# Routed experts in alternating order, with the work around their first items rearranged

## The chip, the core and the metric

The kernel runs on one NeuronCore of a Trainium2 chip. The metric is the device time of one execution in microseconds. Engines are named as in the profile: PE (TensorE, matmuls) with PEld (its weight loads), ACT (ScalarE), DVE (VectorE), POOL (GpSimd) and SP (SyncE, which here issues DMAs).

## The reference, cut to what matters

One layer over 1024 tokens of width 1024: normalised projection, a spatial gating half and a Fourier half, an output projection with the residual, then a mixture of experts:

```python
hn = rms_norm(h, norm2_g[l]).reshape(bsz * s, d)
eidx, gates = route(hn, w_router[l], router_bias[l])      # 8 of 64 experts for each token
routed = routed_experts(hn, eidx, gates, w_gate[l], w_up[l], w_down[l])
# for each expert e and its rows xb:
#   (silu(xb @ w_gate[e]) * (xb @ w_up[e])) @ w_down[e] * gate, added to the tokens' rows
shared = (jax.nn.silu(hn @ ws_gate[l]) * (hn @ ws_up[l])) @ ws_down[l]
h = h + (routed + shared).reshape(bsz, s, d)
return rms_norm(h, final_norm_g)
```

w_gate and w_up are 64 x 1024 x 256, w_down 64 x 256 x 1024, all float32. An expert's weights are 3 MB. The sum over experts does not depend on their order but for rounding.

## The kernel before

**Items.** The kernel counts the tokens of each expert on the chip and cuts each expert's rows into items of at most 128 rows. Table `tab` has two rows of integers, one column for each item: row 0 the item's expert, row 1 twice that number plus 1 if the item is the first of its expert. `ends` holds the number of turns; three items make a turn (`TURN`), and the loops over turns run to that number. With the inputs drawn there are 93 items of 64 experts.

**An item** i goes through these steps. POOL gathers 128 rows from the normed rows in DRAM into `Xg[u]` (L1514) and keeps each row's gate for the item's expert (L1524). PE transposes them (L456). ACT copies them to `xTh` in a rounded float format (L955) and DVE takes the remainder `xTl` (L1332). PE multiplies by gate and up into `ps[3]` in 24 matmuls (L715): high by high, high by rest, rest by high. ACT makes the silu `hs` (L950), DVE multiplies gate, silu and up into `hh` (L1325), PE transposes `hh` (L737), ACT copies `hTh` (L965), DVE takes the remainder `hTl` (L1337), and PE makes the down product in 12 matmuls (L729), which waits for `s_hl`, that is for hTl. ACT copies the result to `ob` (L961), and POOL adds it to the rows in DRAM by an indirect DMA (L1540). PE runs one item ahead: in item i it does the transposes of item i+1's rows, `down(i-1)`, `turn_h(i)` and `gate_up(i+1)`.

**Weights.** SP loads each expert's gate, up (L284, L285) and down (L288) into `raw_gu` and `raw_dn`, which have two places each; a load waits until the expert two before has been split. SP waits in program order: for a landing and for a free place in turn, experts 0, 1, 2, ... ACT copies the weights to the rounded high part (`split_gu` L940, `split_dn` L944), DVE takes the remainders (`rest_gu` L1184, `rest_dn` L1191). In item i gate and up of item i+2's expert are split if that item is the first of its expert, and down of item i+1's expert likewise. On DVE an item is, in this order: gated_h, rest_xT, rest_dn, rest_gu (two parts), rest_h.

**Before the items**, from about 350 us: DVE counts chunks for each expert (`nch`, L1254), PE sums them over experts (L682), DVE derives the item table, PE transposes it (L686) and DVE stores `tab` (L1292). Then for each of the 8 chunks of tokens DVE writes `mark` (L1300) and `pick` (L1302), two chunks deep, and PE multiplies them into the index table in `ps[5]` (L659, `table`). In between PE computes the shared expert's gate and up (`s_gate_up`, L642, eight products of 16 matmuls). Then come eight shared down products of 8 matmuls each (`s_down`, L652), which DVE adds to the residual rows (`y0`, L1380) and SP stores (`store_y0`, L407). The first experts' high and rest parts in `w_gu` place 0 lie over those residual rows, so their splitting waits for the stores (`s_yst`). The loads of experts 0 and 1 are issued right after the output projection.

After the last item, the last three items' rows are added by matmuls with one-hot matrices (L767), and the rows are read back, normed and stored.

Of the kernel before, what the change touches and what calls it, by code (L numbers as in the profile page):

```python
# [23 lines left out]
P = 128  # L24
# [7 lines left out]
NE = 64  # L32
# [30 lines left out]
def build(nc, x, g1, w_in, ln_g, ln_b, wsT, bsT, ga, gb, w_out, g2, w_router, rbias, wg, wu, wd,  # L63
          sg, su, sd, dft_pos, dft_ch, gf, out, hn_d, y_d):
    ctx = ExitStack()
    with ctx:
# [60 lines left out]
        pick = place("pick", [P, 2, TOPK, P], F16, R_AT)  # L127
        rt_a = place("rt_a", [P, NC, NE], F32, R_AT + 4 * KB)
        mark = place("mark", [P, 2, TOPK, TAB], F16, R_AT + 6 * KB + 256)
# [38 lines left out]
        gidx = place("gidx", [P, NC, 8], U32, M_AT + 3 * KB + 256)  # L168
        etop = place("etop", [P, NC, 8], F32, M_AT + 3 * KB + 512)
# [24 lines left out]
        tab = place("tab", [2, TAB], I32)  # L194
# [53 lines left out]
        s_mask, s_chunks, s_cols = sem("mask_ready"), sem("chunks_ready"), sem("item_cols_ready")  # L248
        s_rv, s_pm, s_tab = sem("routing_step"), sem("routing_matmul"), sem("tables_ready")
# [71 lines left out]
        def _(sp):  # L321
# [57 lines left out]
            def load_next_gu(e, at):  # L379
                sp.wait_ge(s_hg, (e - 1) * GU_PARTS)  # L380
                sp.sem_inc(s_turn_sp, 1)
                sp.wait_ge(s_lg, (e - 1) * GU_PARTS)
                sp.sem_inc(s_turn_sp, 1)
                load_gu(sp, e, at)

            def load_next_dn(e, at):
                sp.wait_ge(s_hd, (e - 1) * KF)
                sp.sem_inc(s_turn_sp, 1)
                sp.wait_ge(s_ld, (e - 1) * KF)
                sp.sem_inc(s_turn_sp, 1)  # L390
                load_dn(sp, e, at)
# [60 lines left out]
        def _(pe):  # L452
# [203 lines left out]
            def table(c):  # L656
                pe.wait_ge(s_pick, c + 1)
                for k in range(TOPK):
                    mm = pe.matmul(ps[5][:, 0:TAB], pick[:, c % 2, k, :], mark[:, c % 2, k, :],  # L659
                                   start=(c == 0 and k == 0), stop=(c == NC - 1 and k == TOPK - 1))  # L660
                mm.then_inc(s_table, 1)
# [31 lines left out]
            table(3)  # L693
# [83 lines left out]
            for c in range(4):  # L777
                s_down(c)
            turn_item(0, 1)
            for c in range(4, NC):  # L780
# [3 lines left out]
            pe.wait_ge(s_y0, NC)  # L784
# [256 lines left out]
        def _(dv):  # L1041
# [209 lines left out]

            dv.wait_ge(s_pm, 1)
            for j in range(1, MAXCH):
# [3 lines left out]
            dv.sem_inc(s_chunks, 1)  # L1257
            dv.wait_ge(s_hst[0], 16 * 4)
            dv.wait_ge(s_hst[1], 16 * 4)
            dv.wait_ge(s_t3, NC)  # L1260
            shared_h(0)

            dv.wait_ge(s_pm, 2)
            step(dv.tensor_copy(le[:, 2, :], ps[6][:, 0:NE]))
            step(dv.tensor_scalar(le[:, 0, :], le[:, 2, :], pidx[:, 0:1], None, ALU.is_le))
            step(dv.tensor_tensor(le[:, 1, :], le[:, 0, :], le[:, 2, :], ALU.mult))
            step(dv.tensor_reduce(cols[:, 2:3], le[:, 0, :], AX.X, ALU.add))
            step(dv.tensor_reduce(cols[:, 3:4], le[:, 1, :], AX.X, ALU.max))
            step(dv.tensor_scalar(cols[:, 0:1], cols[:, 2:3], float(NE - 1), None, ALU.min))
            step(dv.tensor_scalar(cols[:, 4:5], cols[:, 3:4], pidx[:, 0:1], None, ALU.is_equal))  # L1270
            step(dv.tensor_scalar(cols[:, 5:6], cols[:, 2:3], float(NE), None, ALU.is_lt))
# [4 lines left out]
            step(dv.tensor_scalar(ends[0:1, 0:1], ps[6][0:1, NE - 1:NE], 1.0, 1.0 / TURN, ALU.add, ALU.mult))  # L1276
# [4 lines left out]
            many((dv.memset(le[:, 3, 0:1], 0.0),  # L1281
                  dv.tensor_scalar(le[:, 3, 1:NE], le[:, 2, 0:NE - 1], float(P), None, ALU.mult)))
# [8 lines left out]
            dv.wait_ge(s_pm, 3)  # L1291
            dv.tensor_copy(tab[0:2, 0:P], ps[7][0:2, 0:P]).then_inc(s_tab, 1)  # L1292

            dv.wait_ge(s_info, 3)

            def slot_marks(c):

                if c >= 2:
                    dv.wait_ge(s_table, c - 1)
                marks = [dv.tensor_scalar(mark[:, c % 2, k, :], count_row[:, :], item8[:, c, k:k + 1], token[:, c:c + 1],  # L1300
                                          ALU.is_equal, ALU.mult) for k in range(TOPK)]
                picks = [dv.tensor_scalar(pick[:, c % 2, k, :], count_row[:, 1:P + 1], place8[:, c, k:k + 1], None,  # L1302
# [15 lines left out]
            shared_h(3)  # L1318
# [27 lines left out]
            def item(i, u, now, coming, final=False):  # L1346
# [38 lines left out]
            second = expert(1)  # L1385
            for c in range(NC):
# [6 lines left out]
            with dv.If(second[0] > 0):  # L1393
                dv.wait_ge(s_yst[1], 16 * 4)
# [261 lines left out]
```

## Time and profile before

| | |
|---|---|
| Median of 3 runs (us) | 1399.57 (1394.94 to 1401.62) |
| The profiled execution (us) | 1403.13 |
| Its span, first to last instruction (us) | 1401.4 |
| PE busy (us, share) | 1333.8, 95% |
| DVE busy | 853.9, 61% |
| ACT busy | 728.3, 52% |
| POOL busy | 464.8, 33% |
| Mean DMA rate (GB/s) | 241, in all 338 MB |
| First and last silu of an item (us) | 449.8, 1360.6 |

Busy time is the union of an engine's instructions; where two lines overlap on PE, neither time is exclusive. Averages over the span mix stages, so the reading goes by the stage of the experts, from about 440 to 1350 us, and by the time between two silus.

### The profile page before, as it was taken

What the parts mean: (1) busy time and instruction counts of PE and PEld (TensorE: products, weight loads), DVE (VectorE), ACT (ScalarE), POOL (GpSimd) and SP (SyncE); (2) the same over time, 40 slices, a digit from 0 to 9 for tenths busy, and PEclk for the clock granted to TensorE, in tenths of its full rate; (3) what the DMA queues carried; (4) which work ended last, traced back from release to release, by engine and by line L of the source; (5) the groups of instructions that cost most, each with busy time, mean ns of one, the idle gap of its engine ahead of it and who ended that gap; (6) DMA issues with size and microseconds to landing.
All of it is one profiled execution on the core that took longest, in us unless ns stands there. A gap on an engine that the chain in (4) does not pass through costs nothing.

```text
span 1401.4 us, 25067 instructions
## 1 busy us (share of the span) xinstructions
PE 1333.8 (95%) x6024; PEld 1042.2 (74%) x6026; DVE 853.9 (61%) x1186; ACT 728.3 (52%) x916; POOL 464.8 (33%) x610
## 2 busy tenths in 40 slices
PE   6999988999999999999999999899998999999996
PEld 5885465888445887888877888787887778888875
DVE  5430543446565667657876556775587666775676
ACT  5321244221011576756765566675577656775663
POOL 2431201000001343434444444443443344344463
PEclk9999998999999999999999999999999999999998
DMA  9604022102306799999998898999899988999899
GB/s 345 183 6 161 4 116 90 46 31 101 133 16 232 248 301 331 316 315 322 315 376 263 254 275 270 369 313 320 250 313 377 372 263 236 332 321 328 249 312 244
DMA packets 88305, 338.01 MB, mean 241 GB/s; under 512 B 12496, under 2 KB 23760, under 8 KB 71504
## 3 DMA queue, kind: packets, MB, share of 16 engines
q1 hardware_dynamic: 60624, 250.53, 46.4%
q0 software_dynamic: 27648, 87.06, 27.0%
q8 instruction: 18, 0.29, 0.1%
q14 instruction: 15, 0.12, 0.0%
HBM read 288.99 MB, written 65.27 MB: 253 GB/s over the span
## 4 chain that ended last, share of the span: by engine, by line
PE 71%; DMA 13%; ACT 5%; DVE 4%; issue 4%; POOL 1%; ACTq 1%; DVEq 1%; SPq 0%; POOLq 0%
PE ps L715 24%; PE ps_out L729 13%; PE ps L607 6%; PE ps L473 6%; DMA raw_dn<-in_w_down 6%; DMA raw_gu<-in_w_up 5%; PE ps L456 5%; PE ps L642 4%; PE ps L509 4%; ACT w_gu L940 3%; DVE w_gu L1184 2%; PE ps L558 2%; DMA ya_in<-y_rows_dram 2%; PE ps_out L624 1%; DVE w_dn L1191 1%
## 5 line engine op out<-in xcount | busy, mean ns | idle before, releaser
L715 PE MATMUL ps<-w_gu,xTh 128*128 x1488 | 468.8, 396 | 4.2 <-DVE xTl L1332 4.2
L1184 DVE TENSOR_TENSOR w_gu<-raw_gu,w_gu (+1 forms) x128 | 292.4, 2290 | 51.6 <-ACT w_gu L940 50.4
L715 PEld LDWEIGHTS ps<-w_gu,xTh 128*128 128x128 f32 x1488 | 273.6, 189 | 58.9 <-issue 5.8
L715 PE MATMUL ps<-w_gu,xTl 128*128 x744 | 291.9, 392 | 0.0
L1540 POOL DMA_INDIRECT y_rows_dram<-ob,idxs x90 | 194.2, 2158 | 252.0 <-ACT ob L961 244.8
L729 PE MATMUL ps_out<-w_dn,hTh 128*128 x744 | 246.9, 414 | 23.3 <-DVE hTl L1337 16.9
L940 ACT ACTIVATE w_gu<-raw_gu (+1 forms) x128 | 245.7, 1920 | 25.7 <-SPq L396 23.4
L729 PEld LDWEIGHTS ps_out<-w_dn,hTh 128*128 128x128 f32 x744 | 136.4, 191 | 60.9 <-issue 35.0
L715 PEld LDWEIGHTS ps<-w_gu,xTl 128*128 128x128 f32 x744 | 140.0, 188 | 29.4
L1332 DVE TENSOR_TENSOR xTl<-ps,xTh 128x512 fp32r<-128x512 f32 x186 | 119.8, 686 | 69.0 <-ACT xTh L955 68.9
L1191 DVE TENSOR_TENSOR w_dn<-raw_dn,w_dn (+1 forms) x128 | 150.4, 1217 | 0.9 <-ACT w_dn L944 0.9
L729 PE MATMUL ps_out<-w_dn,hTl 128*128 x372 | 148.2, 398 | 0.0
L944 ACT ACTIVATE w_dn<-raw_dn (+1 forms) x128 | 128.4, 1056 | 37.9 <-SPq L400 33.6
L1325 DVE SCALAR_TENSOR_TENSOR hh<-hs,gate,ps 128x256 f32<-128x256 f32 x93 | 44.2, 475 | 153.4 <-ACT hs L950 153.4
L955 ACT ACTIVATE xTh<-ps 128x512 fp32r<-128x512 f32 x186 | 101.0, 596 | 62.8 <-PE ps L456 62.8
L1514 POOL DMA_INDIRECT Xg<-hn_rows_dram,idxg x94 | 102.2, 1088 | 76.9 <-POOL idxg L1511 74.8
L950 ACT ACTIVATE hs<-ps 128x256 f32<-128x256 f32 x93 | 35.5, 382 | 142.0 <-PE ps L715 141.8
L456 PEld LDWEIGHTS ps<-ident,Xg 128*128 128x128 f32 x744 | 96.9, 189 | 8.0 <-issue 0.5
L1462 POOL TENSOR_SCALAR rs<-ms 128x1 f32<-128x1 f32 x40 | 21.1, 527 | 234.3 <-ACT junk L810 233.2
L456 PE MATMUL ps<-ident,Xg 128*128 128x128 f32 x744 | 97.2, 274 | 0.0
L1524 POOL COPY gate<-Xg 128x1 f32 x93 | 23.3, 250 | 221.3 <-DVE hh L1325 152.5
L961 ACT ACTIVATE ob<-ps_out 128x1024 f32<-128x1024 f32 x92 | 94.2, 1024 | 0.0
(212 smaller groups left out, 1592.4 us busy)
## 6 DMA issues: line engine op xcount, KB each, us to landing
raw_gu<-in_w_gate SPq DMA_DIRECT2D x64, 1024.0 KB
raw_gu<-in_w_up SPq DMA_DIRECT2D x64, 1024.0 KB
raw_dn<-in_w_down SPq DMA_DIRECT2D x64, 1024.0 KB
y_rows_dram<-zero SPq DMA_DIRECT2D x1, 4608.0 KB, 20.1
x_ring<-in_x SPq DMA_DIRECT2D x8, 512.0 KB, 4.6
w_in_sb<-in_w_in SPq DMA_DIRECT2D x8, 512.0 KB, 9.9
xh<-in_x SPq DMA_DIRECT2D x8, 512.0 KB, 7.0
w_out_sb<-in_w_out SPq DMA_DIRECT2D x1, 4096.0 KB, 12.9
```

The lines of the kernel that those rows point to most:

```text
L456: last = pe.transpose(ps[banks[k // 4]][:, (k % 4) * P:(k % 4 + 1) * P], src[:, k:D:KD], ident[:, :])
L715: mm = pe.matmul(ps[3][:, :], x_[:, k, :], w_gu[:, bass.ds(at, 1), part, :, k, :], start=(k == 0 and part == 0 and x_ is xTh), stop=(k == ...
L729: mm = pe.matmul(ps[6 + half][:, :], h_[:, k, :], w_dn[:, bass.ds(at, 1), part, k, half * 512:(half + 1) * 512], start=(k == 0 and part == ...
L940: act.activation(gu_part(w_gu[:, :, 0, :, :, :], at, m), gu_part(raw_gu, at, m), ACT.Copy).then_inc(s_hg, 1)
L944: act.activation(w_dn[:, bass.ds(at, 1), 0, k, :], raw_dn[:, bass.ds(at, 1), k, :], ACT.Copy).then_inc(s_hd, 1)
L955: act.activation(xTh[:, half * 4:half * 4 + 4, :], ps[1 + half][:, :].rearrange("p (k t) -> p k t", k=4), ACT.Copy).then_inc(s_xa, 1)
L961: act.activation(ob[:, u, :], ps_out[:, :], ACT.Copy).then_inc(s_oa, 1)
L1184: dv.tensor_tensor(gu_part(w_gu[:, :, 1, :, :, :], at, m), gu_part(raw_gu, at, m), gu_part(w_gu[:, :, 0, :, :, :], at, m).bitcast(F32), AL ...
L1191: dv.tensor_tensor(w_dn[:, bass.ds(at, 1), 1, k, :], raw_dn[:, bass.ds(at, 1), k, :], w_dn[:, bass.ds(at, 1), 0, k, :].bitcast(F32), ALU.s ...
L1332: dv.tensor_tensor(xTl[:, part, :], ps[1 + half][:, :].rearrange("p (k t) -> p k t", k=4), xTh[:, part, :].bitcast(F32), ALU.subtract).the ...
L1514: gp.indirect_dma_start(out=Xg[:, u, :], out_offset=None, in_=hn_d[:, :], in_offset=bass.IndirectOffsetOnAxis(ap=idxg[:, u:u + 1], axis=0) ...
L1540: gp.indirect_dma_start(out=y_d[:, :], out_offset=bass.IndirectOffsetOnAxis(ap=idxs[:, u:u + 1], axis=0), in_=ob[:, u, :], in_offset=None, ...
```

## The change

1. The table gets a third row: the experts' numbers in their new order. Row 0 and row 1 now hold the rank of an expert in that order. The rank comes from a key in which the experts with more than one item and those with one are spaced evenly between each other; the chunks are summed by rank (`upto`) instead of by number (`triI`).
2. SP reads the expert's number from row 2 before each load, and the first two loads wait for the table. POOL reads it for the gate's column.
3. `mark` is four chunks deep and lies where the down weights of place 0 come later; `pick` is four deep too, in two tiles.
4. On PE the shared gate and up products and the table's matmuls are interleaved otherwise, and the last shared down product (`s_down(7)`) comes in item 0, after the first gate and up and the transposes of item 1; y0(7) moves with it on DVE.
5. On DVE rest_h comes before rest_gu in each item, and shared_h(3) before the index tables are stored.

```diff
             sp.wait_ge(s_wo, NC)
-            for e in range(2):
-                load_gu(sp, e, 1 - e)
-                load_dn(sp, e, 1 - e)
-
             sp.wait_ge(s_gates, 1)
             sp.dma_start(gates_v[:, :, D:], rt_a[:, :, :]).then_inc(s_gst, 16)
+            sp.wait_ge(s_tab, 1)
+            for j in range(2):
+                e = look(sp, 2, j, NE - 1)
+                load_gu(sp, e, 1 - j)
+                load_dn(sp, e, 1 - j)
...
-                load_gu(sp, e, at)
+                load_gu(sp, look(sp, 2, j, NE - 1), at)
...
-                load_dn(sp, e, at)
+                load_dn(sp, look(sp, 2, j, NE - 1), at)
...
+            pe.wait_ge(s_kinds, 1)
+            pe.matmul(ps[6][:, 0:NE], multi[:, :], tri[0:NE, 0:NE], start=True, stop=True)
+            pe.matmul(ps[6][:, NE:2 * NE], multi[:, :], identb[:, :], start=True, stop=True)
+            pe.matmul(ps[6][:, 2 * NE:2 * NE + 1], multi[:, :], ones[0:NE, 0:1], start=True, stop=True).then_inc(s_pm, 1)
+            s_gate_up(1, 0)
+
             pe.wait_ge(s_chunks, 1)
-            pe.matmul(ps[6][:, 0:NE], nchb[:, :], triI[:, :], start=True, stop=True).then_inc(s_pm, 1)
-            s_gate_up(1, 0)
+            pe.matmul(ps[7][:, 0:NE], nchb[:, :], upto[:, :], start=True, stop=True)
+            pe.matmul(ps[7][:, NE:2 * NE], nchb[:, :], identb[:, :], start=True, stop=True)
+            pe.matmul(ps[7][:, 2 * NE:3 * NE], ones[0:NE, :], upto[:, :], start=True, stop=True)
+            pe.matmul(ps[7][:, 3 * NE:3 * NE + 1], nchb[:, :], ones[0:NE, 0:1], start=True, stop=True).then_inc(s_pm, 1)
+            s_gate_up(1, 1)
 
             pe.wait_ge(s_cols, 1)
-            pe.matmul(ps[7][0:2, 0:P], cols[:, 0:2], ident[:, :], start=True, stop=True).then_inc(s_pm, 1)
-            s_gate_up(1, 1)
+            pe.matmul(ps[6][0:3, 0:P], cols[:, 0:3], ident[:, :], start=True, stop=True).then_inc(s_pm, 1)
             s_gate_up(2, 0)
             table(0)
-            table(1)
             s_gate_up(2, 1)
-            table(2)
-            table(3)
+            for c in range(1, 4):
+                table(c)
             s_gate_up(3, 0)
...
+                if isinstance(i, int) and i == 0:
+                    s_down(NC - 1)
+                if isinstance(i, int) and i == 1:
+                    pe.wait_ge(s_y0, NC)
...
+            many((dv.tensor_scalar(n_multi, ps[6][0:NE, 2 * NE:2 * NE + 1], 1.0, None, ALU.max),
+                  dv.tensor_scalar(kinds[:, 2:3], ps[6][0:NE, 2 * NE:2 * NE + 1], -1.0, float(NE), ALU.mult, ALU.add),
+                  dv.tensor_tensor(key_t[:, 0, :], count_row[0:NE, 0:NE], before, ALU.subtract)))
+            step(dv.tensor_scalar(n_single, kinds[:, 2:3], 1.0, None, ALU.max))
+            many((dv.tensor_scalar(key_t[:, 0, :], key_t[:, 0, :], 0.5, n_multi, ALU.add, ALU.mult),
+                  dv.tensor_scalar(key_t[:, 1, :], before, n_single, None, ALU.mult)))
+            step(dv.scalar_tensor_tensor(out=key_t[:, 1, :], in0=key_t[:, 1, :], scalar=0.25, in1=key_t[:, 0, :],
+                                         op0=ALU.add, op1=ALU.subtract))
...
+            step(dv.tensor_scalar(upto[:, :], key_t[:, 0, :], kinds[:, 3:4], None, ALU.is_ge))
+            dv.sem_inc(s_chunks, 1)
...
+            shared_h(3)
             dv.wait_ge(s_table, NC)
...
-            shared_h(3)
...
                 if isinstance(i, int) and i == 0:
+                    y0(NC - 1)
+                    rest_h(i)
                     dv.wait_ge(s_yst[1], 16 * 4)
+                    with dv.If(coming[0] > 0):
+                        rest_gu(coming[2], coming[1], range(GU_PARTS))
                 else:
                     with dv.If(now[0] > 0):
                         rest_dn(now[2], now[1])
+                if not (isinstance(i, int) and i == 0):
+                    rest_h(i)
                 with dv.If(ahead[0] > 0):
                     rest_gu(ahead[2], ahead[1], range(GU_PARTS))
-                rest_h(i)
...
-                e = look(gp, 0, i, NE - 1)
+                e = look(gp, 2, look(gp, 0, i, NE - 1), NE - 1)
```

## Rows read from the trace of the kernel before

**Rows 1.** Windows: us, busy us of each engine, PEclk, DMA share, GB/s.
```profile
440.00:1352.00 912.00, 886.12 (x4217) 728.35 (x4217) 615.50 (x618) 595.23 (x704) 363.96 (x453) 0.99 0.93 302
...
756.00:862.00 106.00, 105.67 (x516) 87.58 (x515) 63.49 (x68) 62.01 (x78) 43.62 (x55) 1.00 0.87 255
...
1042.00:1099.00 57.00, 50.02 (x235) 40.98 (x234) 44.88 (x42) 41.28 (x46) 20.76 (x25) 0.97 1.03 375
...
1196.00:1263.00 67.00, 66.49 (x321) 54.86 (x320) 47.87 (x49) 46.94 (x55) 27.55 (x35) 1.00 0.99 325
...
440.00:480.00 40.00, 38.11 (x169) 29.62 (x168) 22.64 (x25) 18.78 (x23) 9.04 (x13) 0.96 0.66 233
```

**Rows 2.** One line's or tile's instructions: ns min/median/max; the last, store L407.
```profile
L950 ACT ACTIVATE hs<-ps x93: 360/385/386, 449.8 to 1360.6; 128x256 f32<-128x256 f32 x93
...
L311 ACTq TENSOR_LOAD <-tab x123: 273/285/1192, 413.3 to 1340.8; - x123
...
DMA to landing us min/median/max: 2.6/4.1/9.2
```

**Rows 3.** Timeline of ACT: start us, us, line, operation [idle before <-releaser].
```profile
413.78 3.70 ACT L940 ACTIVATE w_gu<-raw_gu 128x2048 fp32r<-128x2048 f32 x2
...
469.67 0.39 ACT L950 ACTIVATE hs<-ps 128x256 f32<-128x256 f32 x1 [0.48 <-PE ps L715]
...
568.33 0.39 ACT L950 ACTIVATE hs<-ps 128x256 f32<-128x256 f32 x1 [0.48 <-PE ps L715]
...
645.00 0.39 ACT L950 ACTIVATE hs<-ps 128x256 f32<-128x256 f32 x1 [0.48 <-PE ps L715]
...
775.89 0.39 ACT L950 ACTIVATE hs<-ps 128x256 f32<-128x256 f32 x1 [2.29 <-PE ps L715]
...
785.27 0.39 ACT L950 ACTIVATE hs<-ps 128x256 f32<-128x256 f32 x1 [2.37 <-PE ps L715]
...
794.99 0.39 ACT L950 ACTIVATE hs<-ps 128x256 f32<-128x256 f32 x1 [2.29 <-PE ps L715]
...
1042.10 0.39 ACT L950 ACTIVATE hs<-ps 128x256 f32<-128x256 f32 x1 [0.48 <-PE ps L715]
...
1098.81 0.39 ACT L950 ACTIVATE hs<-ps 128x256 f32<-128x256 f32 x1 [0.43 <-PE ps L715]
...
1263.45 0.39 ACT L950 ACTIVATE hs<-ps 128x256 f32<-128x256 f32 x1 [0.48 <-PE ps L715]
...
1302.28 0.39 ACT L950 ACTIVATE hs<-ps 128x256 f32<-128x256 f32 x1 [2.37 <-PE ps L715]
...
1340.72 0.39 ACT L950 ACTIVATE hs<-ps 128x256 f32<-128x256 f32 x1
```

**Rows 4.** Timeline of DVE: table and marks, and one item's remainders.
```profile
376.26 0.28 DVE L1292 CAST tab<-ps_out 2x128 int32<-2x128 f32 x1
...
390.17 1.90 DVE L1300 TENSOR_SCALAR mark<-count_row,item,token 128x136 f16<-128x136 f16 x8 [6.03 <-PE ps L659]
...
778.61 2.35 DVE L1191 TENSOR_TENSOR w_dn<-raw_dn,w_dn  x2
780.87 4.59 DVE L1184 TENSOR_TENSOR w_gu<-raw_gu,w_gu  x2
785.38 0.42 DVE L1337 TENSOR_TENSOR hTl<-ps,hTh 128x256 fp32r<-128x256 f32 x1
```

**Rows 5.** Waits, 480 to 1350 us: who waited <- for whom: us, times, longest.
```profile
PEld ps_out L729 <- issue: 32.2, 60, 3.9
...
ACT w_dn L944 <- SPq L400: 30.9, 16, 4.7
```

**Rows 6.** Timeline of PE at the first shared down product.
```profile
415.68 3.67 PE L652 MATMUL ps<-sd_w,hsT 128*128 128x512 f32 x8 [1.48 <-DVE hsT L1177]
```

**Rows 7.** Chain of waits, 444 to 480 us: start us, us, what.
```profile
444.26 5.50 PE ps L715 x24
...
452.91 7.34 PE ps L715 x24
```

More of the change, by code:

```diff
@@ L168, in build @@
         gidx = place("gidx", [P, NC, 8], U32, M_AT + 3 * KB + 256)
+        key_t = place("key_t", [NE, 4, NE], F32, M_AT)
+        multi = place("multi", [NE, P], BF16, M_AT + 3 * KB + 768)
         etop = place("etop", [P, NC, 8], F32, M_AT + 3 * KB + 512)
@@ L193, in build @@
         cols = place("cols", [P, 12], F32)
-        tab = place("tab", [2, TAB], I32)
+        tab = place("tab", [3, TAB], I32)
+        identb = place("identb", [NE, NE], BF16)
+        upto = place("upto", [NE, NE], BF16)
+        kinds = place("kinds", [NE, 4], F32)
+        pidx1 = place("pidx1", [P, 1], F32)
         ends = place("ends", [1, 8], I32)
@@ L658, in table @@
                 for k in range(TOPK):
-                    mm = pe.matmul(ps[5][:, 0:TAB], pick[:, c % 2, k, :], mark[:, c % 2, k, :],
+                    mm = pe.matmul(ps[5][:, 0:TAB], pick[c // 2 % 2][:, c % 2, k, :], mark[:, c % 4, k, :],
                                    start=(c == 0 and k == 0), stop=(c == NC - 1 and k == TOPK - 1))
@@ L776, in _ @@
             pe.wait_ge(s_hm, 4)
-            for c in range(4):
+            for c in range(5):
                 s_down(c)
             turn_item(0, 1)
-            for c in range(4, NC):
+            for c in range(5, NC - 1):
                 s_down(c)
             gate_up(0, *expert(0))
-            pe.wait_ge(s_y0, NC)
+            pe.wait_ge(s_y0, NC - 2)
             turn_of_items(0, None)
@@ L1260, in _ @@
             dv.wait_ge(s_t3, NC)
+            dv.wait_ge(s_info, 3)
+            dv.wait_ge(s_pm, 2)
+            before, is_multi = ps[6][0:NE, 0:NE], ps[6][0:NE, NE:2 * NE]
+            n_multi, n_single = kinds[:, 0:1], kinds[:, 1:2]
+            many((dv.tensor_scalar(n_multi, ps[6][0:NE, 2 * NE:2 * NE + 1], 1.0, None, ALU.max),
+                  dv.tensor_scalar(kinds[:, 2:3], ps[6][0:NE, 2 * NE:2 * NE + 1], -1.0, float(NE), ALU.mult, ALU.add),
+                  dv.tensor_tensor(key_t[:, 0, :], count_row[0:NE, 0:NE], before, ALU.subtract)))
@@ L1265, in _ @@
+            step(dv.tensor_copy(le[:, 2, :], ps[7][:, 0:NE]))
             step(dv.tensor_scalar(le[:, 0, :], le[:, 2, :], pidx[:, 0:1], None, ALU.is_le))
             step(dv.tensor_tensor(le[:, 1, :], le[:, 0, :], le[:, 2, :], ALU.mult))
+            step(dv.tensor_reduce(cols[:, 8:9], le[:, 0, :], AX.X, ALU.add))
+            step(dv.scalar_tensor_tensor(out=le[:, 0, :], in0=ps[7][:, 2 * NE:3 * NE], scalar=pidx1[:, 0:1],
+                                         in1=count_row[:, 0:NE], op0=ALU.is_equal, op1=ALU.mult))
@@ L1275, in _ @@
             dv.sem_inc(s_cols, 1)
-            step(dv.tensor_scalar(ends[0:1, 0:1], ps[6][0:1, NE - 1:NE], 1.0, 1.0 / TURN, ALU.add, ALU.mult))
+            step(dv.tensor_scalar(ends[0:1, 0:1], ps[7][0:1, 3 * NE:3 * NE + 1], 1.0, 1.0 / TURN, ALU.add, ALU.mult))
             many((dv.tensor_scalar(ends[0:1, 1:2], ends[0:1, 0:1], 1.0, None, ALU.subtract),
@@ L1290, in _ @@
                                          op0=ALU.mult, op1=ALU.add))
[L1291 to L1294 removed]
+            dv.wait_ge(s_pm, 4)
+            dv.tensor_copy(tab[0:3, 0:P], ps[6][0:3, 0:P]).then_inc(s_tab, 1)
             def slot_marks(c):
[L1298 to L1300 removed]
+                if c >= 4:
+                    dv.wait_ge(s_table, c - 3)
+                marks = [dv.tensor_scalar(mark[:, c % 4, k, :], count_row[:, :], item8[:, c, k:k + 1], token[:, c:c + 1],
                                           ALU.is_equal, ALU.mult) for k in range(TOPK)]
[L1302 removed]
+                picks = [dv.tensor_scalar(pick[c // 2 % 2][:, c % 2, k, :], count_row[:, 1:P + 1], place8[:, c, k:k + 1], None,
                                           ALU.is_equal) for k in range(TOPK)]
@@ L1384, in _ @@
             dv.wait_ge(s_tab, 1)
-            second = expert(1)
-            for c in range(NC):
+            for c in range(NC - 1):
                 y0(c)
@@ L1392, in _ @@
             rest_dn(1, 0)
-            with dv.If(second[0] > 0):
-                dv.wait_ge(s_yst[1], 16 * 4)
-                rest_gu(second[2], second[1], range(GU_PARTS))
             turn_of_items(0)
```

37 lines of the change are left out of this document (22 added, 15 removed).

## The prediction

> **What bounds the kernel now.** I read four views in this order. First the windows: over the stage of the routed experts TensorE (PE) is busy for 886 of 912 us, while the DMA share is 0.93 at 302 GB/s [rows 1]. The stage is nearly full on two sides, and only its gaps can be won. Second, the silu of each item on ACT, one per item, 93 of them [rows 2]: a clock for the stage. The inputs send 129 to 234 tokens to 29 experts (two items each, "M") and 71 to 128 to the other 35 (one item, "S"); 58 + 35 = 93. Items are counted from 0. From item 2 to item 90 the silus are 1340.72 - 469.67 = 871.05 us apart, 88 periods [rows 3].
>
> Third, a period when nothing is late: 785.27 - 775.89 = 9.38 us [rows 3]. Fourth, what makes one longer. In the item that begins at 775.89 DVE takes the remainders of a new expert's gate and up (4.59 us) and only then hTl, at 785.38 [rows 4]; that item's down product waits for hTl, and the next period is 794.99 - 785.27 = 9.72 [rows 3]. So an item that splits a new expert's gate and up makes the following period 0.3 us longer, and PE waits 60 times before the down's weight loads, 32.2 us in all [rows 5]. 61 of the 88 periods follow such an item; at 0.33 each, 20.1 us.
>
> The rest, 871.05 - 88 x 9.38 (825.4) - 20.1 = 25.5 us, is waits for weights: ACT waited 16 times for down weights, 30.9 us [rows 5], most of it in runs of S. In the longest run the silus at 1042.10 and 1098.81 are five periods apart, 11.34 us each [rows 3], with the DMA at 375 GB/s; in a stretch of M alone it moved 255 GB/s and PE was full [rows 1]. Bandwidth is idle in one stretch and lacking in another.
>
> **The change, part by part.**
>
> *Alternating order.* The ranking key spaces 29 M and 35 S evenly: M S M S ..., with two S side by side at six places and never two M. A pair M S takes 3 x 9.38 = 28.1 us on PE and needs the weights and rows of two experts: at the S run's pace 2 x 11.34 = 22.7 us, a little more for M's extra rows. The trace has the pattern: items 12 to 19 are the experts S M S M M, and the silus at 568.33 and 645.00 give 9.58 per period [rows 3], which is 9.38 with five late downs in eight: no wait for weights. It also has a double S between M: 1302.28 - 1263.45 = 38.83 us for the four periods from its second S on [rows 3], where two of 9.71 and two of 9.38 make 38.2: 0.7 us lost. With faster items the loads have 1 us less over three items, so a double S costs 0 to 1.7 us; I take 1.1, nearer the row with the faster pace added: 6 x 1.1 = 6.6 us (0 to 10). Gain: 25.5 - 6.6 = 18.9 us.
>
> *Remainder of the silu rows first.* hTl then follows the down remainders (2.35 us from 778.61 [rows 4]) and ACT's hTh, about 5 us into the item, and down(i) finds it ready. DVE's fullest item has these 2.35, 4.59 and 0.42 us and about 1.8 us for hh and xTl, with 0.6 us of waiting for xTh: 9.7 us, 0.3 over the pace. Such an item comes once in three, and the gate-and-up remainder is wanted only in the middle of the next one, so the overrun hides. If it didn't, these periods would stay at 9.7 (0 to 20.1 us gained); I take 20.1, because hTl alone is what the late down waits for.
>
> *The order must be known first.* SP now loads the first two experts of the order after the table, not right after the output projection. The table was ready at 376.5 [rows 4]. DVE gets some 12 small steps before the chunk matmul and 3 behind it, at up to the 0.28 us of the table's own copy [rows 4]; they lie under shared products on PE of 16 matmuls, some 7 us each (8 took 3.67 [rows 6]). One exchange between DVE and PE is added, so the table waits for one product more: about 384. 6.3 MB at 375 GB/s are 17 us: landed by 402, while ACT first splits at 413.78 [rows 3]. Hidden, with 12 us of cover. The six added small matmuls cost PE some 0.6 us (0.3 to 2.7; none longer than one of the 0.46 us that 3.67 / 8 makes [rows 6]).
>
> *Four chunks of marks.* DVE starts them at 384.2 instead of 376.5, some 3.4 us a chunk (marks 1.90 [rows 4], picks a little less), but no longer stands 6.03 us for the first chunks' products [rows 4]. Chunk 3 ends near 398.3, as PE comes to it, the last near 412.5, before PE asks at 413.7. Worth nothing; at worst 1 us.
>
> *shared_h(3) before the index tables.* PE stood 1.48 us for it [rows 6]. This row product no longer waits for the index tables; even with the added matmuls on PE the first down product comes at about 415.3 instead of 415.68. The first gather, 0.9 us later, has one more shared product before its transposes.
>
> *Last shared down product after the first gate and up.* Gate-up 0 comes 0.4 us and one shared product (some 3.5 us) earlier and ends at 445.9 instead of 449.8 [rows 7], and s_down(7) fills the wait before gate-up 1, which then ends near 456 instead of 460.3; before, it took 7.34 us at the lower clock, against 5.50 for gate-up 0 [rows 7]. But y0(7) is now ready at 451.4 (445.9 + 0.9 transposes + 3.5 + about 1.1), its store lands about 4.1 us later [rows 2], and DVE waits for that (456.0) before the 4.6 us of remainders of the next expert, with gated_h(1) and xTl(2) queued behind them. PE gets hh(1) at 461.2 (0.5 more) and xTl(2) at 462.5 (1.3 more), where its own work would be there at 459.9 (456 + transposes 0.9 + down 2.8 + 0.2). Silu 2 comes at 468.0, or up to 1.84 us later if the gap slows the clock again as at 452.91; I take 468.9 against 469.67 [rows 3]: 0.8 us gained (-1 to +2). TensorE's granted clock was 0.96 from 440 to 480 us, after this idle piece, and 1.00 in the stretches without one [rows 1].
> The Trainium skill, "TensorE: Matmul & The Clock Gate", Part 1, says that an idle array falls back to the lower clock and that activity releases it; the trace agrees at 452.91. [...]
>
> *Table row 2.* SP reads the expert's number before each load, POOL one more for each gate column; such a read took 0.29 us on ACT [rows 2]. SP's load has two items of time, POOL waits in every item anyway. It shows only in the last two items, where POOL's gate columns stand in the chain to the end: 0.6 us, against which the last expert no longer stands in a run of four S (about 1 us). Tail: 0 (-1 to +1).
>
> **The sum**, in the profiled execution: silu 2 at 468.9; 88 x 9.38 = 825.4; double S 6.6; silu 90 at 1300.9 instead of 1340.72; tail as before. Gain 39.8 us. That execution took 1403.1 us (span 1401.4 and 1.7 around it), 3.6 over the median of the runs; from the median, 1399.6 - 39.8 = 1359.8, say 1360. Own range 1348 to 1373.
>
> **Rivals.**
> A. DVE takes hTl's place: the 4.59 us of remainders end later, and hh or xTl of the next item is late. The 20.1 us are not gained: 1380. For it: 9.7 us of DVE in the fullest item. Against: PE needs hh only after a down product, some 2.5 us on.
> B. The waits for weights don't go but spread: the DMA share was 0.99 in 1196 to 1263, a mixed stretch at 325 GB/s [rows 1], so loads may land just in time everywhere. Half to all of 18.9 us not gained: 1369 to 1379. Against: the share is also 0.87 at 255 GB/s, so it doesn't tell the capacity; 375 does.
> A and B together: 1399, no change.
> C. Slower. Each S between two M waits once for its weights, since SP's order of waits is strict (gate and up landed, only then the down load): the mean wait before was 30.9 / 16 = 1.93 us [rows 5]. 35 x 1.93 = 67.6 us in place of 25.5 is 42.1 more, less the 20.9 of the hTl order and the start: 1421. It decides from (25.5 + 20.9) / 35 = 1.3 us per S. Against: the S between M in items 12 to 19 cost nothing.
> D. The change doesn't do what it says: the order comes out as before, and only the hTl order and the start act, 1379.
>
> **Chances.** Forecast 0.58; A 0.13; B 0.12; D 0.03; A with B 0.08; C 0.06. Within 0.5% (7 us, about what a measurement tells from no change): 0.08. Slower: 0.06. Faster: 0.86. Range 1346 to 1386, which takes in A, B and D.
>
> **What would show it.** Right: periods of 9.38 also after a split; PE's 60 waits at the down's loads nearly gone; ACT's waits for landed weights under 10 us, at six places; 832 us between the silus of items 2 and 90; the DMA near 317 GB/s all through (302 x 912 / 869); first split no later than 414. Wrong: periods of 9.7 with hTl early (A), ACT waiting in each triple of items (B, C), or a first split waiting for its load.

## The result, and the profile after

The changed kernel takes 1382.1 us (median of 4 runs, 1378.2 to 1384.5) against 1399.7 before (median of 4): ratio 0.9868, 95% interval 0.985 to 0.9886. It is 17.6 us faster where 39.8 were forecast; the range began at 1346 and ended at 1386, so the time is inside it, but less than half of the gain came.

The silus of items 2 and 29 to 31 and what ACT waits for in item 31, in ACT's timeline of the kernel after (start us, us, line, operation, idle before and its releaser; silu and splits of gate and up and of down now have lines 969, 959 and 963). They answer to [rows 3]:

```profile
468.17 0.38 ACT L969 ACTIVATE hs<-ps 128x256 f32<-128x256 f32 x1
...
729.62 0.39 ACT L969 ACTIVATE hs<-ps 128x256 f32<-128x256 f32 x1
...
731.47 1.92 ACT L959 ACTIVATE w_gu<-raw_gu  x1
...
739.00 0.39 ACT L969 ACTIVATE hs<-ps 128x256 f32<-128x256 f32 x1 [2.37 <-PE ps L730]
...
742.80 1.92 ACT L959 ACTIVATE w_gu<-raw_gu  x1 [1.83 <-SPq L404]
...
749.49 0.39 ACT L969 ACTIVATE hs<-ps 128x256 f32<-128x256 f32 x1
...
756.37 2.01 ACT L963 ACTIVATE w_dn<-raw_dn  x2 [2.69 <-SPq L408]
758.48 0.39 ACT L969 ACTIVATE hs<-ps 128x256 f32<-128x256 f32 x1
```

Silu 2 is at 468.17; forecast was 468.9. Silu 90 is at 1321.56, so the 88 periods take 853.4 us where 832.0 were forecast. From there to the end of the span it is 61.2 us, 0.6 more than before. Against the forecast's own terms the whole miss lies in the 88 periods.

A triple (two items of an M, one of an S) shows it: 739.00 - 729.62 = 9.38, then 10.49, then 8.99, together 28.86 instead of 28.14. Of the 14 triples that have no double S in them, 12 take 28.6 to 29.1 us, the other two 28.25 and 28.4. The six groups of seven items with a double S take 2.5 to 4.8 us over 7 x 9.38 = 65.66. ACT stands twice for SP: 1.83 us before the split of gate and up in the M expert's second item, 2.69 us before that of the down weights in the S item. The waits over 480 to 1320 us (us in total, times, longest) answer to [rows 5]; PE's 60 waits before the down's weight loads are gone from the list. ACT's waits for SP grew to 145 us; in the kernel before they were 53 us over the same stretch, 30.6 for down and, what the prediction left out, 22.5 for gate and up. The first line is of the kernel before, the others of the kernel after:

```profile
ACT w_gu L940 <- SPq L396: 22.5, 13, 4.0
...
ACT w_dn L963 <- SPq L408: 78.4, 24, 6.1
DVE hTl L1379 <- ACT hTh L984: 78.1, 33, 3.8
ACT w_gu L959 <- SPq L404: 66.7, 33, 2.7
...
PEld ps L730 <- issue: 25.1, 36, 1.6
PE ps L730 <- DVE xTl L1374: 14.5, 26, 1.3
```

Windows of the kernel after (us, busy us of PE, PEld, DVE, ACT, POOL, granted clock, DMA share, GB/s), answering to [rows 1]. In the three later stretches the rate is even now, 309 to 323 GB/s where it was 255 to 375, and the DMA share is 0.97 or more; at the start of the stage, 440 to 480 us, it is 0.59:

```profile
440.00:480.00 40.00, 38.15 (x178) 29.99 (x177) 24.39 (x28) 21.24 (x26) 14.51 (x16) 1.00 0.59 209
756.00:862.00 106.00, 103.91 (x504) 85.87 (x503) 72.91 (x75) 72.88 (x87) 47.74 (x56) 1.00 0.99 323
1042.00:1099.00 57.00, 56.32 (x272) 46.42 (x272) 39.54 (x40) 37.96 (x45) 27.80 (x30) 1.00 0.97 309
1196.00:1263.00 67.00, 66.60 (x327) 55.39 (x327) 48.20 (x48) 45.29 (x55) 32.21 (x35) 1.00 0.99 323
```

In the kernel before, TensorE's clock had cost something too. These are windows of the kernel before inside three of its long periods; the granted clock, the third number from the end, is between the two levels of 1.00 (2.4 GHz) and 0.50 (1.2 GHz), each time after PE had stood for a part of the 3 to 4 us before (busy 1.19 of 3.00 us in 703 to 706):

```profile
706.00:711.00 5.00, 4.58 (x15) 3.60 (x15) 4.10 (x6) 2.96 (x4) 1.38 (x3) 0.66 1.05 318
894.00:902.00 8.00, 6.71 (x19) 5.28 (x20) 7.03 (x8) 3.80 (x6) 2.83 (x4) 0.57 1.04 360
1089.00:1093.00 4.00, 4.00 (x12) 3.05 (x12) 3.56 (x4) 1.79 (x1) 1.17 (x2) 0.59 1.06 293
```

The missing shares of these 17 us add up to 6.8 us (0.34 x 5 + 0.43 x 8 + 0.41 x 4). That is an estimate of what the lower clock cost there. The prediction had counted it among its 25.5 us of waits for weights. In the kernel after the granted clock is 1.00 over 480 to 1320 us, so up to 6.8 us of the gain may have come this way; no run separates it.

What ACT waits for is in the chain of waits of the kernel after around the M expert's second item (start us, us, what):

```profile
737.13 2.30 DVE w_gu L1203
...
739.61 1.49 SPq L318
...
741.56 0.34 SPq L291
...
742.00 0.41 SPq L292
...
742.92 0.26 SPq L318
...
743.62 0.38 SPq L295
```

SP gives the landing signals in program order. In a step it waits for DVE's remainders of the expert before (they end at 739.43), reads the next expert's number (1.49 us), issues its two loads, and only then passes on that the gate and up of the expert in the other place have landed. ACT starts at 742.80, right behind the second issue. So this wait doesn't show that the weights came late.

### The profile page after: what moved, and what is told of

It is laid out like the page before. It is cut to its first block, busy times and chain, and to the rows that moved or that the text cites. A ratio compares the mean times of both kernels' runs of the same rounds, so it can differ in the third digit from the quotient of the medians.

```text
span 1382.8 us, 25986 instructions
## 1 busy us (share of the span) xinstructions
PE 1321.7 (96%) x6030; PEld 1033.6 (75%) x6032; DVE 859.0 (62%) x1203; ACT 722.8 (52%) x916; POOL 521.9 (38%) x610
## 3 DMA queue, kind: packets, MB, share of 16 engines
q0 software_dynamic: 27648, 87.06, 27.8%
## 4 chain that ended last, share of the span: by engine, by line
PE 57%; DVE 9%; DMA 9%; issue 9%; ACT 5%; SPq 5%; DVEq 4%; ACTq 1%; POOL 0%; POOLq 0%
PE ps L730 18%; PE ps L615 7%; PE ps L481 7%; PE ps_out L744 6%; DMA raw_dn<-in_w_down 5%; DVE w_gu L1203 5%; PE ps L650 4%; PE ps L517 4%; PE ps L464 4%; SPq L318 3%; DMA ya_in<-y_rows_dram 2%; ACT w_gu L959 2%; DVE w_dn L1210 2%; PE ps L566 2%; DVEq L318 2%
## 5 line engine op out<-in xcount | busy, mean ns | idle before, releaser
L730 PEld LDWEIGHTS ps<-w_gu,xTh 128*128 128x128 f32 x1488 | 273.8, 188 | 81.4 <-issue 27.1
L1583 POOL DMA_INDIRECT y_rows_dram<-ob,idxs x90 | 222.3, 2470 | 235.2 <-ACT ob L980 213.7
L1203 DVE TENSOR_TENSOR w_gu<-raw_gu,w_gu (+1 forms) x128 | 290.4, 2287 | 11.9 <-issue 11.8
L744 PE MATMUL ps_out<-w_dn,hTh 128*128 x744 | 242.1, 407 | 1.6 <-ACT ob L980 1.6
L963 ACT ACTIVATE w_dn<-raw_dn (+1 forms) x128 | 128.2, 1053 | 87.3 <-SPq L408 78.4
L744 PEld LDWEIGHTS ps_out<-w_dn,hTh 128*128 128x128 f32 x744 | 133.2, 189 | 27.0 <-issue 1.9
L1567 POOL COPY gate<-Xg 128x1 f32 x93 | 41.1, 442 | 159.9 <-DVE hh L1367 102.2
L1379 DVE TENSOR_TENSOR hTl<-ps,hTh 128x256 fp32r<-128x256 f32 x93 | 39.0, 419 | 84.9 <-ACT hTh L984 84.9
```

The lines of the kernel that those rows point to most:

```text
L730: mm = pe.matmul(ps[3][:, :], x_[:, k, :], w_gu[:, bass.ds(at, 1), part, :, k, :], start=(k == 0 and part == 0 and x_ is xTh), stop=(k == ...
L744: mm = pe.matmul(ps[6 + half][:, :], h_[:, k, :], w_dn[:, bass.ds(at, 1), part, k, half * 512:(half + 1) * 512], start=(k == 0 and part == ...
L963: act.activation(w_dn[:, bass.ds(at, 1), 0, k, :], raw_dn[:, bass.ds(at, 1), k, :], ACT.Copy).then_inc(s_hd, 1)
L1203: dv.tensor_tensor(gu_part(w_gu[:, :, 1, :, :, :], at, m), gu_part(raw_gu, at, m), gu_part(w_gu[:, :, 0, :, :, :], at, m).bitcast(F32), AL ...
L1583: gp.indirect_dma_start(out=y_d[:, :], out_offset=bass.IndirectOffsetOnAxis(ap=idxs[:, u:u + 1], axis=0), in_=ob[:, u, :], in_offset=None, ...
```

## The experiments

Three theories. Theory 1: the chain over SP just shown sets the pace. Theory 2: the DMA engines do; rows and weights together fill them. Theory 3, formed after the first two rounds: both, one behind the other, so that taking away one alone shows only the other. Ratios are to the kernel before, run on the same chip; times in us of different experiments can come from different chips, on which the kernel before took 1398.6 to 1400.4 us.

**hTl first, alone.** The kernel before, with one edit on DVE:

```diff
+                rest_h(i)
                 with dv.If(ahead[0] > 0):
                     rest_gu(ahead[2], ahead[1], range(GU_PARTS))
-                rest_h(i)
```

> The kernel before with one part of the change: DVE takes hTl before the remainders of gate and up. Theory 1 (SP's program order: the signal that an expert's weights have landed is given only after the next load is issued, and that load waits for DVE's remainders of the expert before): the remainders end about 0.4 us later in the item, which is hidden in stretches of M and is paid in runs of S; 8 to 18 us faster than before, 1382 to 1391. Theory as predicted (hTl alone): 20 us faster, 1379. Theory 3 (the late hTl cost nothing, the order of DVE's pieces is neutral): 1399.

Measured 1397.8 us, ratio 0.998 (0.9964 to 0.9996): 2.6 us, not 20. In stretches of M the late period fell from 9.7 to 9.55 only. The chain of waits of this kernel there has the late down gone (2.80 us right behind the transposes), but a gate-up of 5.67 us:

```profile
764.09 0.88 PE ps L456 x8
764.97 2.80 PE ps_out L729 x12
767.77 0.22 PE ps L737 x2
767.99 5.67 PE ps L715 x24
...
777.56 5.46 PE ps L715 x24
```

DVE's timeline says why: the remainders of gate and up now end at 764.57, hh and xTl come behind them, and PE's gate-up needs xTl, which ends at 767.72.

```profile
762.28 2.29 DVE L1184 TENSOR_TENSOR w_gu<-raw_gu,w_gu  x1
764.54 0.48 DVE L1325 SCALAR_TENSOR_TENSOR hh<-hs,gate,ps 128x256 f32<-128x256 f32 x1
766.43 1.29 DVE L1332 TENSOR_TENSOR xTl<-ps,xTh 128x512 fp32r<-128x512 f32 x2 [1.41 <-ACT xTh L955]
```

And weights were waited for instead: over 480 to 1320 us ACT's waits for down weights went from 30.6 to 61.1 us, those for gate and up from 22.5 to 33.1. So DVE partly took hTl's place (rival A), and most of the rest went into waits for weights.

**hTl last again, in the kernel after.** The same lines the other way round.

> The kernel after with hTl behind the remainders of gate and up again, as before. If hTl first is worth its 0.33 us per expert in the new order, 1402. Theory 1: the gain was spent in the chain over SP, so little changes: periods of 9.7, 9.7, 9.4 (28.8 us a triple, as now 28.87), 1380 to 1386.

Measured 1408.6 us, ratio 1.0059 (1.0039 to 1.0079): 26 us slower than the kernel after, and slower than the kernel before. My expectation under theory 1 (1380 to 1386) was wrong; the other one, 1402, was nearer and still 7 us short. The piece that moved is worth 2.6 us alone and 26 in the new order. The late period is 10.2 us long and the one behind it 10.3. My reading is that the split comes late over SP, with it DVE's remainders, and that hTl stands behind these, so that PE pays the same lateness a second time; the run with hTl last and an early read, below, bears it out. Its waits:

```profile
PEld ps_out L744 <- issue: 46.2, 58, 1.5
ACT w_gu L959 <- SPq L404: 38.6, 32, 2.5
PE ps_out L744 <- DVE hTl L1379: 33.3, 30, 1.3
```

**SP reads early.**

```diff
             def load_next_gu(j, at):
+                e = look(sp, 2, j, NE - 1)
                 sp.wait_ge(s_hg, (j - 1) * GU_PARTS)
...
-                load_gu(sp, look(sp, 2, j, NE - 1), at)
+                load_gu(sp, e, at)
```

and the same in load_next_dn.

> The kernel after, with SP's read of the expert's number ahead of the two waits of each load instead of behind them. Theory 1: the read (1.49 us before the load of gate and up once in three items) leaves the chain from DVE's remainders to ACT's next split; ACT's wait of 1.8 us falls to 0.3, a triple from 28.87 to about 28.2: 1362 to 1368. Theory 2 (the DMA engines are at their limit, weights land just in time): 1382, unchanged.

Measured 1384.8 us, ratio 0.9891 (0.987 to 0.9912): no gain over the kernel after. The wait for gate and up is gone as expected (66.7 to 11.9 us), but the one for down grew from 78.4 to 103.1. ACT in the S item of a triple:

```profile
746.72 1.02 ACT L982 ACTIVATE ob<-ps_out 128x1024 f32<-128x1024 f32 x1
751.91 2.01 ACT L965 ACTIVATE w_dn<-raw_dn  x2 [4.16 <-SPq L410]
```

The down load had been issued at 736.89, 15 us earlier. In the chain of waits of this kernel over 480 to 1320 us, summed by line, the transfer of the down weights has 29.0% (8.8% in the kernel after, where L318 on SP, the table read, has 4.7% and DVE's remainders of gate and up 7.9%). L318 on SP is down to 1.5%, and the transfer has taken its place:

```profile
by line: DMA raw_dn<-in_w_down 29.0%; PE ps L732 28.0%; PE ps_out L746 11.7%; issue 7.2%; DVE w_gu L1205 4.4%; PE ps L466 4.3%; DVE w_dn L1212 2.6%; SPq L318 1.5%; DVEq L318 1.3%; ACTq L318 1.3%; DVE xTl L1376 0.9%; PE ps L754 0.9%; DVEq L1
```

**Landing first.** SP passes on a landing before it waits for the next load's place, with the read still in the chain:

```diff
-                load_next_gu(t * 2 + 1, 0)
                 gu_landed(1, t + 1)
-                load_next_dn(t * 2, 1)
+                load_next_gu(t * 2 + 1, 0)
                 dn_landed(0, t)
+                load_next_dn(t * 2, 1)
```

> The kernel after, with SP's order changed: it passes on that an expert's weights have landed before it waits for the place of the next load, instead of after it. Theory 1: ACT no longer waits for DVE's remainders of the expert before, though the read stays; triples of 28.2 us, 1360 to 1366, and ACT's waits for SP nearly gone outside the six double S. Theory 2 (bandwidth): 1382.

Measured 1386.0 us, ratio 0.9896 (0.9878 to 0.9913). Waits for gate and up 3.0 us in all, for down 94.4. Theory 1 as the only cause falls with these two runs; theory 2 expected just this.

**Two thirds of the weights.** No up weights are loaded; the gate weights come in two DMAs of 0.5 MB and are split in the up weights' place too, so the kernel no longer computes the layer; the work of PE, ACT and DVE is the same.

```diff
-            eng.dma_start(raw_gu[:, at, 1, :, :], wu[e].rearrange("(p k) f -> p k f", k=KD)).then_inc(s_gu_in[at], 16)
+            eng.dma_start(raw_gu[:, at, 0, 4:8, :], wg[e].rearrange("(p k) f -> p k f", k=KD)[:, 4:8, :]).then_inc(s_gu_in[at], 16)
```

> The kernel after with a third of the weight traffic left out: no up weights are loaded, the gate weights (in two DMAs of half the size) are split in their place, so the result is another one; ACT, DVE and PE do the same work, and the order of all waits is the same. Theory 2 (the DMA engines are the bound; each item's rows cost them about 4 us and each expert's weights 8, so a triple M M S costs 28 us against PE's 28.1, and weights land late): waits for down weights gone, triples of 28.14 to 28.3, 1358 to 1366. Theory 1 (SP's program order and late issue alone): the wait for gate and up before the second M item stays at 1.8 us, 28.9 a triple, 1380.

Measured 1381.1 us, ratio 0.9872 (0.9848 to 0.9897): the time of the kernel after, at 242 GB/s instead of 316. Triples of 28.9 us, gate and up waited for 66.1 us, down 76.6. Theory 2 as the only cause falls too.

**Half of the added rows' traffic.** The indirect DMA of L1583 adds 512 of the 1024 columns of each row, at other places; again another result, with the same work on PE, ACT and DVE.

```diff
-                gp.indirect_dma_start(out=y_d[:, :], ...
-                                      in_=ob[:, u, :], ...
+                gp.indirect_dma_start(out=y_d[:, :].rearrange("r (a f) -> (r a) f", a=2), ...
+                                      in_=ob[:, u, 0:D // 2], ...
```

> The kernel after with half of the traffic of the added rows: the indirect DMA adds 512 of each row's 1024 columns, at other places, so the result is another one; weights and waits are unchanged. Theory 2: about 1 us of DMA time less per item, 3 per triple: triples near 28.2 to 28.5, 1362 to 1370. Theory 1: 1382. If the row traffic's cost is per row and not per byte: 1382 as well, and the run of two thirds of the weights decides.

Measured 1357.7 us, ratio 0.9694 (0.9664 to 0.9723), better than theory 2 expected. The two effects come together here. The rows' DMA queue fell from 41.1% to 27.8% of the DMA engines' time. And SP's read in the chain became shorter. The reads at the same place of two triples (the M expert's second item; ns min/median/max, start), the kernel after:

```profile
L318 SPq TENSOR_LOAD <-tab x1: 1486/1486/1486, 739.6 to 739.6; - x1
...
L318 SPq TENSOR_LOAD <-tab x1: 1475/1475/1475, 768.5 to 768.5; - x1
```

and with half of the added rows:

```profile
L318 SPq TENSOR_LOAD <-tab x1: 791/791/791, 730.8 to 730.8; - x1
...
L318 SPq TENSOR_LOAD <-tab x1: 787/787/787, 758.9 to 758.9; - x1
```

This run alone can't tell which of the two gave the 24 us; it showed that both limits meet in the row traffic, and led to theory 3.

**Down before gate and up.** With the early read, SP issues an expert's down load before the next expert's gate and up:

```diff
-                load_next_gu(t * 2 + 1, 0)
                 gu_landed(1, t + 1)
                 load_next_dn(t * 2, 1)
+                load_next_gu(t * 2 + 1, 0)
                 dn_landed(0, t)
```

> The kernel after with SP's number read early and with the load of an expert's down weights issued before the next expert's gate and up instead of behind them. Theory 2a (late issue: down of the M expert waits on SP for a place of gate and up that comes free 5 us later, though its own is free): the wait for down weights in the S item (3 to 4 us with the early read alone) falls to under 1 and triples come to 28.2, 1362 to 1368. Theory 2b (total DMA time): only another load is late, 1378 to 1388.

Measured 1470.1 us, ratio 1.0485 (1.0445 to 1.0525), far slower, which no theory expected in this size. In S items the gate-and-up load now stands behind DVE's remainders of down and is issued 7.4 to 12 us into the item instead of 0.8; ACT waited 148.5 us for down weights, up to 10.0 us at a time. A load held back by a place that isn't free delays every load behind it.

**hTl last, SP reads early.** The alternating order without the hTl order and without the read in the chain.

> The kernel after with hTl last, as in the kernel before, and SP's read early: the alternating order without the hTl order and without the read in the chain. If the 26 us that hTl last cost in the new order came over the read behind DVE's remainders (chain over SP), 1380 to 1388. If hTl last costs PE its 0.33 us per expert whatever SP does: 1400 to 1405.

Measured 1383.5 us, ratio 0.9889 (0.9864 to 0.9914). Beside hTl last with the read in the chain (1408.6) the read costs 25 us (24 by the two ratios); beside the early read with hTl first (1384.8) the hTl order is worth nothing. The two versions of equal time don't lose it in the same place, though. Here the late down is back, in nearly every triple two periods of 9.7 and one of 9.4, 28.8 us, and PE waits 60 times before the down's weight loads:

```profile
PEld ps_out L746 <- issue: 18.9, 60, 0.8
ACT w_dn L965 <- SPq L410: 60.9, 28, 5.0
```

With hTl first and the early read those waits of PE are gone, and ACT waits 103.1 us for down weights instead of 60.9. What PE no longer loses, the loads take.

**Early read and two thirds of the weights.** The two edits, each of which had changed nothing.

> SP's read early, and a third of the weight traffic left out (no up weights loaded, the result is another one). Each of the two alone gave 1381 to 1385. Theory 3 (two limits behind one another: first the chain DVE's remainders, SP's slow read, ACT's split; behind it the landing of the down weights): with both gone the triples come to 28.14, 1356 to 1362, and ACT's waits for SP fall under 20 us in all. If something else sets the pace (DVE's own work and reads): 1378 to 1385.

Measured 1362.3 us, ratio 0.9742 (0.9721 to 0.9762). From silu 2 (465.32) to silu 90 (1297.67) it is 832.35 us. The forecast had 832.0, but that they are so near is chance: the forecast's 6.6 us over 825.4 are double S, while here the 6.9 us lie in nearly all triples (0.2 us each, in periods of 9.5 to 9.6), and the six groups of seven with a double S are 0.4 to 0.8 us over 65.66. It is also not the changed kernel, for a third of its weights is left out. Waits over 480 to 1320 us:

```profile
ACT w_dn L965 <- SPq L410: 37.7, 27, 1.8
DVE hTl L1381 <- ACT hTh L986: 24.6, 28, 1.9
PEld ps L732 <- issue: 4.4, 21, 0.4
ACT w_gu L961 <- SPq L406: 0.7, 2, 0.5
PE ps L732 <- DVE xTl L1376: 0.2, 1, 0.2
```

The down waits left are 1.8 us at the longest, and PE hardly waits. In the chain of waits over the same stretch the weights' transfers have no share left, and PE's four lines have 96.8%. Theory 3 stands, with two misses in its own terms: the waits of 37.7 us are above the 20 I had set, and 1362.3 is at the upper end of 1356 to 1362. What it shows is that the traffic is the second limit. Whether that is the 16 DMA engines' time or the memory behind them, no run tells apart.

**Both reads ahead.** All traffic. `look` for both loads of a step stands before the step's first wait.

```diff
+            def loads(j, at, fills, before_fills):
+                eg = look(sp, 2, j, NE - 1)
+                ed = look(sp, 2, j - 1, NE - 1)
+                free_gu(j)
+                load_gu(sp, eg, at)
+                gu_landed(1 - at, fills)
+                free_dn(j - 1)
+                load_dn(sp, ed, 1 - at)
+                dn_landed(at, before_fills)
```

> All traffic. SP reads both numbers of a step (next gate and up, and down) before the step's first wait, so that the down load follows the landing signal without a read between. Against the early read alone, where down of the M expert was issued 3.9 us into the item and landed 3 us late in the next, the issue comes 1.4 us earlier. Theory 3: down lands about 1.4 us earlier, triples of 28.2 to 28.6, 1366 to 1376. If the DMA rate alone sets the landing: 1380 to 1385.

Measured 1385.9 us, ratio 0.9911 (0.9893 to 0.993). The down load is issued 2.6 us into the item instead of 3.9, and the wait for it is as long as before (107.2 us in all). In ACT's timeline near 750 us the down weights' split starts at 751.70, with the down load issued at 736.79 and the gate-and-up load in front of it, in the same queue, at 735.39; in the early-read kernel it is 751.91, with 736.89 and 734.20. The expected 1366 to 1376 was wrong, and 1380 to 1385 nearly right. An earlier issue does not bring the load in earlier. Whether it waits for the gate-and-up load in front of it or for the rest of the traffic, this run doesn't tell.

**Natural order.** In the kernel after, the ranks are the experts' own numbers:

```diff
-            step(dv.tensor_scalar(upto[:, :], key_t[:, 0, :], kinds[:, 3:4], None, ALU.is_ge))
+            step(dv.tensor_copy(upto[:, :], triI[:, :]))
```

> The kernel after, with the experts' order set back to 0, 1, 2, ...: table row 2, SP's reads, the hTl order and the start are as in the kernel after. The hTl order alone gave 1398. If the alternating order is what makes the gain of 18 us, this is 1395 to 1405, the slow reads making it no better than hTl first alone. If the start and the hTl order carry it, 1382 to 1388.

Measured 1398.3 us, ratio 1.0002 (0.999 to 1.0015). Without the alternating order the rest of the change brings nothing that can be measured, and by the run with hTl last the order without the hTl move costs time. So with the read in the chain the two edits are worth something only together; with the early read the order does without the hTl move (1383.5).

**Landing first, both reads ahead.** `gu_landed` moved to the top of `loads`, behind the reads.

> As the kernel with both reads ahead, and besides a step passes on the landing of gate and up before it waits for the next load's place. The chain from DVE's remainders to ACT's next split is then cut wholly. Theory 3: waits for gate and up nearly none, waits for down as with both reads ahead, since its load still follows the next gate and up load: 1362 to 1376. If down lands as late as with landing first and the slow read (1386): 1380 to 1386.

Measured 1389.5 us, ratio 0.9934 (0.9917 to 0.9952), where 1362 to 1376 or 1380 to 1386 had been expected, somewhat slower than the kernel after: waits for gate and up 2.6 us, for down 111.0. Why it is slower than with both reads ahead alone (1385.9) was not looked into. None of the versions with all the traffic beat the kernel after.

## Why the prediction was wrong, by its own steps

*Alternating order: the step that failed.* The term for what the loads still cost was 6.6 us over 88 x 9.38 = 825.4; measured are 853.4 - 825.4 = 28.0. Behind it stood what a pair M S asks of the loads, set at "the S run's pace 2 x 11.34 = 22.7 us, a little more for M's extra rows" against PE's 28.1. An M has two items, and each item has a whole gather and a whole addition of rows. The view of the DMA queues (packets, MB, share of 16 engines' time) of the kernel before in the S run, 1042 to 1099 us, with 5 experts and 5 items:

```profile
q1 hardware_dynamic: 2926, 16.50, 70.1%
q0 software_dynamic: 1476, 4.86, 32.8%
```

70.1% of 57 us is 40.0 us, 8 for each of the five experts' weights (7.6 if counted by bytes, since 16.50 MB are 5.2 times an expert's 3.15); 32.8% is 18.7 us, 3.7 for an item's rows. A pair is then 2 x 8 + 3 x 3.7 = 27.1 us of the DMA engines (26.3 by bytes), 94 to 96% of PE's 28.1, not 81%. In the kernel after, over 480 to 1320 us:

```profile
q1 hardware_dynamic: 33400, 187.19, 57.2%
q0 software_dynamic: 25041, 78.26, 41.1%
```

57.2% of 840 us for 187.19 MB makes 8.1 us for the 3.15 MB of an expert; 41.1% over 840 / 9.7 = 87 items makes 4.0 us. A pair: 2 x 8.1 + 3 x 4.0 = 28.2 us, as much as PE needs. I took the rate (375 GB/s) for the capacity and dismissed the share (0.99 at 325) in rival B; but rows move fewer bytes than weights in the same engine time, 227 against 390 GB/s by these lines, so a rate from a stretch with few rows doesn't carry over.

These microseconds are an estimate and no fixed prices. With a third less weights 1 MB of weights took 2.8 us and 1 MB of rows 4.8, instead of 2.6 and 4.4. And from 739 to 741 us of the kernel after, with no weights under way, rows alone made a share of 95% at 98 GB/s:

```profile
q0 software_dynamic: 48, 0.20, 94.9%
```

So a share near 1 doesn't prove by itself that no more could be moved. That the traffic matters beside the chain over SP is shown by the pair of runs with two thirds of the weights: 1381.1 with the read in the chain, 1362.3 without, against 1384.8 with the early read and all weights.

Of the 28.0 us, some 17 lie in the triples, for which the prediction had nothing: the 14 without a double S are 0.64 over 28.14 on average, and there are 26 if each group of seven with a double S counts for two. The double S was sized too small as well. The six groups are 3.8, 3.2, 2.6, 4.8, 2.7 and 2.5 us over 65.66; less two triples each (1.3) that leaves 1.2 to 3.5 for a double S, 2.0 on average and 12 in all, where 1.1 and 6.6 were forecast, the upper bound being 10. The items 12 to 19 of the kernel before, on which "no wait for weights" rested, have 5 new experts in 8 items; the new order has 64 in 93, 10% more for each item.

*"SP's load has two items of time": wrong.* The load has, but the signal that stands behind it in SP's program has not. The table read was priced at 0.29 us, the median, and hidden, though the same row [rows 2] has one of 1.19 us. It took 1.37 to 1.53 us 28 times between 480 and 1320 us, once in nearly every triple, in the gate-and-up step, and stood in the chain. It costs 25 us with hTl last (1408.6 against 1383.5), and nothing that shows with hTl first and all the weights (1382.1 against 1384.8), since the landing of the down weights is then behind it; with two thirds of the weights it costs 19 (1381.1 against 1362.3).

*Remainder of the silu rows first: 20.1 us forecast, 2.6 measured alone.* The late down did go. Rival A's counter, the slack of hh, was right for hh and overlooked xTl behind it; in the natural order half of the 0.33 us was lost there (periods of 9.55), and waits for weights took most of the rest. In the new order the edit is worth 26 us while the read is in the chain, and nothing without it.

*The start: right in what PE waits for, in part by luck in the time.* PE waited for hh and xTl behind DVE's remainders, as worked out, and gate-up 2 began at 461.24 (forecast 462.5). It ended at 466.95. Silu 2 came only at 468.17 (forecast 468.9), because ACT was splitting down weights from 466.28 on (2.00 us), a wait that the prediction doesn't have. ACT's first split came at 413.68, before at 413.78. The loads behind the table, the marks and the added matmuls cost nothing visible, and with the natural order all of it together, with reads and hTl, came to 0. The clock's part: the granted clock was 1.00 from 440 to 480 us, so this start paid none of the 1.84 us; taking half of it was 0.9 too much, and the whole would have been 1.84 too much. Before, PE stood 1.72 us in one piece before gate-up 1; now it stands 0.82 us before the transposes of hh and 1.00 us before gate-up 2.

*Tail: right*, 61.2 against 60.7.

In all: rivals A and B each came true in part, and with B I had named the place where to look (1369 to 1379 for it alone). That the time is near the 1380 of rival A is chance. Its sign, periods of 9.7 with hTl early, did not show; "ACT waiting in each triple of items", the sign of B and C, did.

## What to carry to other kernels

Before spreading transfers evenly, add up the transfer engines' time queue by queue for a whole repeating pattern, rows and weights each with its own microseconds, and compare with the compute of the same pattern; a GB/s from one stretch does not carry to another mix. A share near 1 is a sign and no proof; here it took a run without the chain and without a third of the weights to show both limits. Where one queue both issues loads and passes on landings, its program order is a chain of its own, and anything added to it, even a table read, is paid by whoever waits for the signals. And a small gain on the bound engine counts only where nothing else is within that gain of being the bound: here PE, the chain over SP and the traffic lay within 3% of each other, so that two edits worth 0 each, on top of the change, were worth 20 us together.

## What the runs showed of the hardware that was not expected

SP's read of one number of the table from SBUF took 0.28 us at the median, but 1.49 us at one place of the triple, and DVE's read there 1.26 us. Both began 3.9 us after POOL had started the addition of an item's rows to DRAM. With half of that traffic, at the same distance from the start of the addition, they took 0.79 and 0.9 us; with two thirds of the weights SP's still took 1.5 us. In the 2 us of the long read that began at 739.6 the rows' packets were slow as well, 98 GB/s at a share of 0.95. Long reads are not new: in the kernel before, DVE's took 0.32 us at the median and up to 1.43. So the long read goes with the rows, not with the weights; that rests on one profiled run of each, and the mechanism was not looked into.
